# Moving 1/rms out of the rows and onto the banks in the last feed-forward part of a two-layer FP32 backbone kernel

## The reference, cut to what matters

```python
def rmsnorm(x, g):
    y = x32 * lax.rsqrt(jnp.mean(x32 * x32, axis=-1, keepdims=True) + EPS)
    return (y * g)
def modulate(z, shift, scale):
    return z * (1.0 + scale) + shift
def swiglu(z, w_in, w_out):
    gate, up = jnp.split(z @ w_in, 2, axis=-1)
    return (jax.nn.silu(gate) * up) @ w_out
# last part, l = 1
h = h + m[5] * mix_out(...)
h = h + 0.5 * m[8] * swiglu(modulate(rmsnorm(h, ffn2_norm_g[l]), m[6], m[7]), ffn2_w_in[l], ffn2_w_out[l])
return rmsnorm(h, final_norm_g)
```

## Time and profile before

| what | value |
|---|---|
| median of 3 runs | 1570.7 us (1564.53 to 1571.11) |
| the profiled execution's own time | 1571.65 us |
| its span, first to last instruction | 1569.9 us |
| PE busy | 1550.9 us, 99% of the span |
| DVE busy | 1054.0 us, 67% |
| ACT busy | 682.6 us, 43% |
| DMA | 262.53 MB, mean 167 GB/s |
| PE's part of the chain that ended last | 94% |

### The profile page before, as it was taken

The page is one execution under the profiler, slowest core; times in us unless marked ns, Lnnn a source line. Parts: engine busy times, 40 slices in busy tenths (PEclk is TensorE's granted clock), DMA queues, the critical chain, the costliest instruction groups (busy, mean ns, idle before and its releaser), DMA issues.

```text
span 1569.9 us, 22187 instructions
## 1 busy us (share of the span) xinstructions
PE 1550.9 (99%) x8796; PEld 1339.8 (85%) x8796; DVE 1054.0 (67%) x1305; ACT 682.6 (43%) x1112; POOL 159.1 (10%) x193
## 2 busy tenths in 40 slices
PE   8999999999999999999999999999999999999997
PEld 6888888889888988888888898888888897999997
DVE  5777874794868567874378477784368578965553
ACT  4434433333784343433233353343332369654452
POOL 0011110022100201110002200011002211000011
PEclk9999999999999999999999999999999999999999
DMA  9577664665322257663367446764367523465562
GB/s 367 198 212 206 201 186 137 206 203 129 107 81 80 82 188 208 199 186 98 121 205 212 114 153 190 217 197 115 98 203 229 154 89 127 135 201 187 188 200 82
DMA packets 79468, 262.53 MB, mean 167 GB/s; under 512 B 13201, under 2 KB 13457, under 8 KB 78353
## 3 DMA queue, kind: packets, MB, share of 16 engines
q1 hardware_dynamic: 71696, 248.70, 49.3%
q0 software_dynamic: 7680, 12.59, 5.0%
HBM read 247.62 MB, written 1.05 MB: 158 GB/s over the span
## 4 chain that ended last, share of the span: by engine, by line
PE 94%; DVE 2%; ACT 1%; DMA 1%; issue 0%; SPq 0%; POOL 0%; POOLq 0%; DVEq 0%; ACTq 0%
PE bank L446 84%; PE bank L568 2%; PE bank L574 2%; PE bank L570 2%; DMA ada_head<-head_w 1%; PE bank L737 1%; PE bank L711 1%; PE bank L709 1%; PE bank L710 1%; PE bank L523 0%; PE bank L739 0%; DVE w_lo L1173 0%; PE bank L462 0%; PE bank L454 0%; DVE l_q L1441 0%
## 5 line engine op out<-in xcount | busy, mean ns | idle before, releaser
L867 ACT ACTIVATE w_hi<-raw 128x1024 fp32r<-128x1024 f32 x317 | 335.9, 1060 | 722.1 <-PE bank L446 707.1
L1173 DVE TENSOR_TENSOR w_lo<-raw,w_hi 128x1024 fp32r<-128x1024 f32 x317 | 388.3, 1226 | 313.3 <-ACT w_hi L867 312.8
L446 PE MATMUL bank<-z_hi,w_hi 128*128 128x512 f32 (+1 forms) x1480 | 537.7, 363 | 1.8 <-DVE w_lo L1173 1.4
L446 PE MATMUL bank<-z_lo,w_hi 128*128 128x512 f32 (+1 forms) x1480 | 534.7, 361 | 0.0
L446 PE MATMUL bank<-z_hi,w_lo 128*128 128x512 f32 (+1 forms) x1480 | 534.5, 361 | 0.0
L446 PEld LDWEIGHTS bank<-z_hi,w_hi 128*128 128x128 f32 x1480 | 278.5, 188 | 46.0 <-DVE w_lo L1173 1.8
L446 PEld LDWEIGHTS bank<-z_hi,w_lo 128*128 128x128 f32 x1480 | 279.8, 189 | 42.4
L446 PEld LDWEIGHTS bank<-z_lo,w_hi 128*128 128x128 f32 x1480 | 278.4, 188 | 42.8 <-issue 1.0
L446 PE MATMUL bank<-h_hi,w_hi 128*128 128x512 f32 (+1 forms) x770 | 267.4, 347 | 0.0
L446 PE MATMUL bank<-h_hi,w_lo 128*128 128x512 f32 (+1 forms) x770 | 266.9, 347 | 0.0
L446 PE MATMUL bank<-h_lo,w_hi 128*128 128x512 f32 (+1 forms) x770 | 266.9, 347 | 0.0
(11 more groups left out here) (187 smaller groups left out, 1405.6 us busy)
## 6 DMA issues: line engine op xcount, KB each, us to landing
raw<-weights SPq DMA_DIRECT2D x320, 512.0 KB, 4.1
ada_raw<-ada_w SPq DMA_DIRECT2D x128, 512.0 KB, 4.3
ada_head<-head_w SPq DMA_DIRECT2D x8, 1024.0 KB, 19.1
up_acc<-up_acc POOLq DMA_DIRECT2D x20, 256.0 KB, 6.5
down_acc<-down_acc POOLq DMA_DIRECT2D x12, 256.0 KB, 6.2
up_acc<-up_acc POOLq DMA_DIRECT2D x40, 64.0 KB, 6.1
res<-x_t SPq DMA_DIRECT2D x4, 512.0 KB, 5.1
down_acc<-down_acc POOLq DMA_DIRECT2D x24, 64.0 KB, 5.5
```

What stands on the lines that cost most here:

```text
L446: m = pe.matmul(bank[:, to], w, x[:, k, at], start=start and i == 0, stop=stop and i == 2, skip_group_check=True)
L867: act.activation(w_hi[:, r, :], raw[:, r, :], ACT.Copy).then_inc(hi_ready, 1)
L1173: dve.tensor_tensor(w_lo[:, r, :], raw[:, r, :], w_hi[:, r, :].bitcast(F32), ALU.subtract).then_inc(lo_ready, 1)
```

## The change

In this one norm (n = 5) the rows that PE streams are no longer divided by rms and no longer shifted. ACT writes `z_hi` = round(h G) straight from `res` and DVE makes `z_lo` from `res` as well; both can run as soon as a row's residual is there. The shift goes in as two more columns behind the 256 token columns of `z_hi` and `z_lo` (`SHIFTS`; two since latent and context lie side by side), so that every matmul of the part runs over 258 columns (`ALONE_SHIFTED`) and column 256 of each bank holds the shift times the weights. 1/rms is computed beside that, and the factor row (256 times r, then two ones) is kept in `factors`, which lies in `ada_raw`. DVE multiplies each bank by it; ACT takes Silu from `scr` with the shift's column as bias, and one DVE instruction adds the shift's column to the up half and multiplies by the gate half.

```diff
+SUMS_AT = 6
+SHIFTS = slice(LAT0 + SEQ, LAT0 + SEQ + 2)
+        factors = ada_raw[:, ADA_RING - 1, 0:SEQ + 2]
+        ALONE_SHIFTED = (slice(0, SEQ + 2), slice(LAT0, LAT0 + SEQ + 2))
 # PE, first_slots of this part
-                    z = row_cols(n, 0)
+                    to, z = ALONE_SHIFTED
                     pe.wait_ge(hi_ready, base + 3)
+                    pe.wait_ge(lo_ready, base + 2)
+                    pe.wait_ge(shift_lo_ready, 1)
+                    pe.wait_ge(res_ready, HID0 + KD * (n - 1) + 6)
                     for k in range(KD):
...
+                        if k == SUMS_AT:
+                            pe.wait_ge(sqsum_ready, pool_sums(n))
+                            sums(ss_bank(n, 0), 2, 0, True, False)
+                            pe.wait_ge(sq_ready, KD * (n + 1))
+                            sums(ss_bank(n, 0), 1, 0, False, True).then_inc(ss_done, 1)
...
                     m.then_inc(slot_done, 1)
+                    norm_spread(n, 0)
                     return
 # PE, out_stage
                 if split_rows(n):
                     rows_by_stream()
-                else:
-                    norm(n)
 # ACT, up_stage
-                    if q % 2 == 0:
+                    if q % 2 == 0 and streams(w) == 1:
+                        act.wait_ge(normed_ready, jj + 1)
+                        act.activation(scr[:, q // 2, 0:w], scr[:, q // 2, 0:w], ACT.Silu,
+                                       bias=scr[:, q // 2, w:w + 1]).then_inc(silu_ready, 1)
 # ACT, out_stage of layer 1: the new rows and the end
+                    def scaled_high(d):
+                        act.wait_ge(res_ready, HID0 + KD * (n - 1) + d + 1)
+                        act.activation(z_hi[:, d, row_cols(n, 0)], res[:, d, 0:SEQ], ACT.Copy,
+                                       scale=n_gain[:, n, d, 0:1]).then_inc(z_hi_ready, 1)
+                    act.activation(z_hi[:, :, SHIFTS], n_shift[:, n, :, :], ACT.Copy).then_inc(shift_hi_ready, 1)
...
+                    act.wait_ge(slot_done, after)
+                    split_hi(after + 3, 3)
                     root(n)
-                    split_hi(after + 2, 2)
-                    act.wait_ge(slot_done, after)
-                    norm(n, after)
+                    act.wait_ge(bcast_done, halves(n) + 1)
+                    act.activation(factors[:, 0:SEQ], spread_bank(n, 0)[:, 0:SEQ], ACT.Copy).then_inc(factors_ready, 1)
+                    act.activation(warm[:], ones[:, 0:1], ACT.Silu)
 # DVE, up_stage
+                    if streams(w) == 1 and q % 2 == 0:
...
+                        dve.tensor_tensor(scr[:, q // 2, 0:w + 2], pa[q][:, 0:w + 2], factors, ALU.mult).then_inc(normed_ready, 1)
+                    if streams(w) == 1 and q % 2 == 1:
+                        dve.wait_ge(hid_lo_ready, HID_LO0 + j)
+                        link(dve.tensor_tensor(scr[:, 2, 0:w + 2], pa[q][:, 0:w + 2], factors, ALU.mult))
+                        dve.wait_ge(silu_ready, j + 1)
+                        dve.scalar_tensor_tensor(scr[:, 2, 0:w], scr[:, 2, 0:w], scr[:, 2, w:w + 1], scr[:, q // 2, 0:w],
+                                                 ALU.add, ALU.mult).then_inc(hid_ready, 1)
 # DVE, out_stage of layer 1
+                    def scaled_low(d):
+                        dve.wait_ge(z_hi_ready, z_piece(n, d, 0))
+                        dve.scalar_tensor_tensor(z_lo[:, d, row_cols(n, 0)], res[:, d, 0:SEQ], n_gain[:, n, d, 0:1],
+                                                 z_hi[:, d, row_cols(n, 0)].bitcast(F32), ALU.mult, ALU.subtract).then_inc(z_ready, 1)
+                    dve.wait_ge(shift_hi_ready, 1)
+                    dve.tensor_tensor(z_lo[:, :, SHIFTS], n_shift[:, n, :, :], z_hi[:, :, SHIFTS].bitcast(F32),
+                                      ALU.subtract).then_inc(shift_lo_ready, 1)
...
+                    dve.reciprocal(tokr[:, 0:2], tok[:, 0:2]).then_inc(rstd_ready, 1)
+                    dve.wait_ge(slot_done, after)
+                    split_lo(after + 3, 3)
 # POOL, before the last norm
+                    pool.memset(factors[:, SEQ:SEQ + 2], 1.0).then_inc(factor_ones, 1)
```

More of the change, by code:

```diff
@@ L579, in first_slots @@
                 if not both:
-                    z = row_cols(n, 0)
+                    to, z = ALONE_SHIFTED
                     pe.wait_ge(hi_ready, base + 3)
+                    pe.wait_ge(lo_ready, base + 2)
+                    pe.wait_ge(shift_lo_ready, 1)
+                    pe.wait_ge(res_ready, HID0 + KD * (n - 1) + 6)
                     for k in range(KD):
-                        row(k, 0, (0, 1))
                         c = slice(k * P, (k + 1) * P)
-                        for x in (z_hi, z_lo):
-                            pe.matmul(banks[2][:, COLS[0]], w_hi[:, 2, c], x[:, k, z], start=(k == 0 and x is z_hi),
-                                      stop=False, skip_group_check=True)
+                        pe.wait_ge(z_hi_ready, z_piece(n, k, 0))
+                        for q in (0, 1):
+                            for i, w in enumerate((w_hi, w_lo)):
+                                pe.matmul(banks[q][:, to], w[:, q, c], z_hi[:, k, z], start=(k == 0 and i == 0),
+                                          stop=False, skip_group_check=True)
+                        pe.matmul(banks[2][:, to], w_hi[:, 2, c], z_hi[:, k, z], start=(k == 0), stop=False, skip_group_check=True)
+                        pe.wait_ge(z_ready, z_piece(n, k, 0))
+                        for q in (0, 1):
+                            m = pe.matmul(banks[q][:, to], w_hi[:, q, c], z_lo[:, k, z], start=False,
+                                          stop=(k == KD - 1), skip_group_check=True)
+                            if k == KD - 1:
+                                m.then_inc(slot_done, 1)
+                        pe.matmul(banks[2][:, to], w_hi[:, 2, c], z_lo[:, k, z], start=False, stop=False, skip_group_check=True)
+                        if k == SUMS_AT:
[3 more added lines that the diff above has]
+                            sums(ss_bank(n, 0), 1, 0, False, True).then_inc(ss_done, 1)
@@ L610, in up_stage @@
                 n = 3 * l + 2 * f
-                part = all_of(streams(dft(n)))
+                part = BOTH if streams(dft(n)) == 2 else ALONE_SHIFTED
                 def slot(i, p):
@@ L1323, in norm @@
                         z_low(k, s)
-                        if not split_rows(n) and k == KD - 1:
-                            split_lo(base + 2, 2)
-                            split_lo(base + 3, 3)
                         if split_rows(n) and s == 0:
```

51 lines of the change are left out of this document (34 added, 17 removed).

## The result

| | before | after |
|---|---|---|
| median, run beside each other on the same chips | 1564.81 us (19 runs, 1563.70 to 1571.11) | 1571.97 us (19 runs, 1570.35 to 1574.74) |
| profiled execution | 1571.65 us, span 1569.9 | 1572.21 us, span 1570.4 |

The change makes the kernel slower. The ratio over all runs is 1.0034, with a 95% interval from 1.0024 to 1.0045; the two medians are further apart (7.16 us, 0.46%), since before has some slower runs, as told next. The forecast was 1570.4 us, a change of -0.29 us.

The account below looks back on a forecast made before the run. PE was taken as the bound, busy 99% of the span; -5.16 + 0.13 + 0.06 + 0.74 + 0.55 + 0.02 + 2.57 + 0.80 = -0.29 us from a 1570.7 median gave 1570.4 us, range 1565.0 to 1574.0.

Parts of the forecast that it names:

- The start: Up projection's first matmul at 1364.45: the norm's 5.16 us gap removed, 0.13 us given back for small shift instructions.
- The first three slots: PE's 72 matmuls: 0.06 us for wider columns, 0.74 for sums, 0.55 for the spread, issued at 1373.81.
- The new wait: Before slot 4, PE stalls 2.57 us behind the spread and ACT's work; slot 4 starts at 1379.86.
- The line of hops: From spread to slot 4: serial steps on PE, ACT and DVE, including table load and rounding, 6.05 us in sum.
- The clock: Rival: the clock falls in the bare wait before slot 4, losing 1.7 us of work, giving 1572.1 us; 12%.
- ACT and DVE: In the other 40 slots, DVE's extra 0.42 + 0.48 us per pair stays covered and ACT's instructions are unchanged: cost nothing.
- The other 40 slots: From slot 4 on, 960 matmuls each 0.83 ns longer for two more columns: 0.80 us.
- The rival for it: 258 columns cost more than two columns: another 4.8 ns on each of 1056 matmuls, 5.1 us, giving 1575.5 us; 8%.
- if the distance between starts grows by more than 1 ns: Stated sign that the forecast is wrong, for PE's matmuls, expected 118.3 ns between starts after slot 4.
- The base: Starting time of the whole kernel: the execution's own 1571.65 us, with the median of runs shown 0.95 lower, 1570.7.
- like columns and not like loads: PE's matmul spacing read as set by streamed columns, 10.8 ns over them at 256 and 512, so 0.80 us was kept.

Follow-up runs that it names:

- experiment 4: The changed kernel with ACT's Silu table load moved ahead of its wait for the spread: 1569.04 us, ratio 1.0017.
- experiment 3: The changed kernel with seven throwaway matmuls on PE between slots 3 and 4: 1570.97 us, ratio 1.0027.
- experiments 2: The changed kernel with 256 columns everywhere, the shift left out and a constant column in its place: 1564.73 us, ratio 0.999.
- experiment 1: The kernel before with every matmul of the last up projection over 258 columns, the two extra results unread: 1571.79 us, ratio 1.0027.
- experiment 5: The kernel before, unchanged, run once more with a profile: 1565.25 us.
- The scan: The kernel before with slots 4 to 43 in ten groups of differing start column, width and bank place, output not the reference's: 111.7 to 121.6 ns between starts.
- experiment 11: The kernel before with 258 columns in the first three slots of the last up projection alone: 1571.16 us, ratio 1.0027.
- experiment 12: The changed kernel with 256 columns, the shift left out, and Silu's table load ahead of ACT's wait for the spread: 1561.39 us, ratio 0.9985.
- experiment 16: The changed kernel with Silu's table load early and rows and shift columns from column 80 instead of 112: 1569.67 us, ratio 1.0016.

## Why the prediction was wrong, step by step

- **The start.** Forecast 1364.45, measured 1364.02, at once behind the output projection. The delay of 0.13 us for the shift's small instructions did not arise, and the projection itself went at the quicker pace: 0.45 us for four steps before 1363.90.
- **The first three slots.** The sums stand in the stream as forecast (0.79 us, forecast 0.74), and the spread is issued at 1373.60 instead of 1373.81. It holds slot 3 up 0.36 us, not 0.55.
- **The new wait.** Forecast 2.57 us with slot 4 at 1379.86; measured 2.2 us and 1379.26. From the spread it is 5.66 us instead of 6.05. The line of hops was right, each term within 0.2 us (the largest miss is the step from the spread to the factor copy, 0.64 instead of 0.82); experiment 4 takes 1.5 us out of it by its largest avoidable term. The gain at slot 4 is 1.69 us, 0.6 more than forecast.
- **The clock.** The rival's mechanism came true in the profiled run: about 1.5 us. It had 12%. In experiment 3, with PE kept busy, it doesn't come; how often it comes with the bare wait is known only roughly, from the clocks named there.
- **ACT and DVE.** Their extra work stayed covered. PE waits for neither again in the part.
- **The step that failed: "The other 40 slots. 960 matmuls with 0.83 ns more: 0.80 us."** The measured price of 258 columns is 120.83 - 113.33 = 7.5 ns a matmul: 7.2 us over these 960, which experiments 2 and 4 show by the block of 1488. With the first 96 it would be 7.9 us by the same price; experiment 1, where all 1056 are wider, shows 7.4. I took the slope between 256 and 512 columns and laid a straight line through an interval in which I had no row. The two points were read with an error of their own, since windows count matmuls across their edges: by the starts it is 117.78 and 226.67 ns, so what is left over the bare columns is 11.1 and 13.3 ns, not the same 10.8. The rival for it had the right mechanism and 8%; the condition I named for it, "if the distance between starts grows by more than 1 ns", is what came. The size in that rival was short: 4.8 ns against 7.5, or against 3.05 if the base is the slower pace of before.
- **The base was wrong too.** The forecast stood on 1571.65, an execution of the upper level, and on a median of three that fell in the same level. The pace of 117.5 ns in the earlier trace rows was the slower of two. The row that could have told is the earlier trace rows: twelve matmuls of the same shape at 112.7 ns. I named it as a spread, and didn't ask whether the whole stream could run at it.
- **Luck.** The median of after, 1571.97, lies only 1.6 us from the forecast. That is no merit of the sum: the base stood 5.9 us too high (1570.7 against 1564.81) and the change was forecast 7.45 us too low (-0.29 against +7.16), and the two nearly cancel.

The account against a lower-level execution of before: 1565.25 (experiment 5), slot 4 earlier by 1.86 (it starts at 1381.12 there), 960 x 7.5 ns = 7.20 more, 1.51 for the clock (177.64 against 176.13 for the block). Sum 1572.10; the profiled run of after took 1572.21. Against the upper level the same terms hide each other: slot 4 earlier by 1.69, 960 x (120.83 - 117.78) = 2.93 more, the clock 1.51 more, and the down projection's 528 matmuls at 113.33 instead of 117.78, 2.35 less; sum +0.40, measured +0.56.

The prediction said that the 10.8 ns over the bare columns at 256 and at 512 look "like columns and not like loads". The scan contradicts that: 224, 240 and 256 columns go at 111.7, 113.3 and 113.3 ns (254 stands out with 118.3), where 32 columns by the slope of 0.417 ns would be 13.3. Below 256, then, the number of streamed columns isn't what sets the pace. The Trainium skill, "TensorE: Matmul & The Clock Gate", section on the back-to-back gap, has the spacing set by weight load and matmul together, and gives N/2.4 + 2.5 ns for a matmul by itself. The near-flat part, 1.6 ns for 32 columns, agrees with the first; neither gives the measured step of 6.7 to 7.5 ns from 256 columns at their quicker pace to 258.

**What stays open.** Why 256 columns of z from an odd multiple of 16 are quicker than 254, 258 or another start: start and width of the streamed operand matter and the place in the bank does not, and more I can't tell. Even start and width don't fix the pace by themselves. What picks one of the paces where a stream begins again after a break is open; the one idea tried (experiment 11) fell. Not tried was a form that keeps 256 columns throughout by streaming normalized rows once they are there; the room for it is at most that of experiment 12, 3.1 us.

## What to carry to other kernels

Before widening a stream that fills PE, measure the distance between starts at the new width and start column; a slope between two far widths says nothing of the next one, and seven nanoseconds on a thousand matmuls outweigh a removed gap of five microseconds. See in which level a kernel's runs lie, and of which one the profile is, before taking a median of three as its time. Don't take a pace from one stretch of one execution for that of the next, either: experiment 16 did. When a wait is moved onto an engine, put what doesn't need it (here a table load) ahead of it; that gave 2.9 us here.

## What was not expected of the hardware

- A stream of 256-column matmuls has two steady paces, 113.33 and 117.78 ns at a granted clock of 1.00, between executions of one program (6.6 us in 1512 matmuls) and between stretches of one execution (experiments 2 and 5). The changes seen came at breaks in the stream.
- The pace depends on the start column of the rows streamed from z: 113.33 or 117.78 ns from 112, 120.00 from 0 or 96.
- 254 columns at 118.3 ns (one group of 96) are slower than 256 at 113.3; 264 at 120.0 cost no more than 258.
- One bare wait of 2.2 us between full stretches was followed by about 3.4 us at half clock in one execution and by none in another.
